# Block order of the last attention's input projection: q0 q1 s0 q2 s1 q3 s2 s3 in place of q0 s0 q1 s1 q2 s2 q3 s3

## What is computed

```
h = rms_norm_2(x, od_norm_w)
proj = h @ od_w_in                                  # 2048 -> 4608
q, k, v, gate = split(proj, [2048, 2304, 2560])     # 32 query heads of 64, 4 key/value heads, 32 heads of gates
q = rope(rms_norm_2(q by heads, q_norm_w), pos)     # k the same
o = windowed_attention_with_sinks(q, k, v, sinks)   # window 128: each block of 128 sees itself and the block before
x = x + (o * silu(gate)) @ od_w_out                 # 2048 -> 2048
```

## Time and profile before

| | |
|---|---|
| median of 3 runs | 1894.64 us (1894.14 to 1895.88) |
| profiled execution | 1893.72 us, its span 1891.9 us |
| TensorE busy | 1879.0 us, 99% of the span, granted clock 1.0 |
| VectorE busy | 1256.7 us, 66% |
| ScalarE busy | 999.7 us, 53% |
| last attention | units 557 to 644, about 1555 to 1846 us of the span |

### The profile page before, as it was taken

How to read it: one execution, slowest core, us unless ns; L and a number is a source line. 1 busy time by engine, 2 the same in 40 slices (tenths; PEclk the granted TensorE clock), 3 DMA queues, 4 the chain that set the end, 5 groups by cost and what they waited for, 6 DMA issues and landing times.

```text
span 1891.9 us, 22459 instructions
## 1 busy us (share of the span) xinstructions
PE 1879.0 (99%) x8563; PEld 1546.8 (82%) x8563; DVE 1256.7 (66%) x1847; ACT 999.7 (53%) x1378; POOL 14.4 (1%) x32
## 2 busy tenths in 40 slices
PE   9999999999999999999999999999999999999999
PEld 7888888888888888888888888888888888877777
DVE  6676567676666566665466776755766677767765
ACT  6777554554444344443444455654555555566663
POOL 0001000000000000000000000000000000000000
PEclk9999999999999999999999999999999999999999
DMA  9667764786666666666666786666676687554565
GB/s 326 201 191 179 206 184 135 225 256 191 197 191 194 196 189 190 198 193 195 191 195 193 219 268 192 193 196 178 189 212 192 195 254 219 175 170 150 167 188 173
DMA packets 212363, 375.85 MB, mean 199 GB/s; under 512 B 14672, under 2 KB 35968, under 8 KB 212256
## 3 DMA queue, kind: packets, MB, share of 16 engines
q1 hardware_dynamic: 211008, 371.65, 64.0%
q0 software_dynamic: 816, 2.11, 0.9%
q10 hardware_dynamic: 432, 0.66, 0.1%
HBM read 361.76 MB, written 12.60 MB: 198 GB/s over the span
## 4 chain that ended last, share of the span: by engine, by line
PE 94%; DVE 3%; ACT 2%; issue 1%; DMA 0%; SPq 0%; DVEq 0%; ACTq 0%
PE g L1185 30%; PE g L1187 30%; PE g L1186 30%; PE m L1119 1%; DVE wl L1652 1%; ACT wh L1375 1%; DVE TW L1652 0%; PE ob L1263 0%; DVE st L1661 0%; PE m L1345 0%; PE m L1245 0%; DVE st L1655 0%; ACT A L1513 0%; DVE A L1655 0%; PE m L1127 0%
## 5 line engine op out<-in xcount | busy, mean ns | idle before, releaser
L1652 DVE TENSOR_TENSOR wl<-raw,wh 128x1024 fp32r<-128x1024 f32 (+1 forms) x660 | 802.5, 1217 | 561.4 <-ACT wh L1375 558.6
L1375 ACT ACTIVATE wh<-raw 128x1024 fp32r<-128x1024 f32 (+1 forms) x661 | 696.3, 1054 | 719.0 <-PE g L1187 713.9
L1185 PE MATMUL g<-wh,xh 128*128 128x512 f32 x1886 | 741.8, 393 | 1.9 <-DVE wl L1652 1.9
L1187 PE MATMUL g<-wh,xl 128*128 128x512 f32 x1886 | 734.6, 390 | 0.0
L1186 PE MATMUL g<-wl,xh 128*128 128x512 f32 x1886 | 734.2, 389 | 0.0
L1185 PEld LDWEIGHTS g<-wh,xh 128*128 128x128 f32 x1886 | 354.1, 188 | 80.0 <-DVE wl L1652 4.3
L1187 PEld LDWEIGHTS g<-wh,xl 128*128 128x128 f32 x1886 | 354.0, 188 | 74.2
L1186 PEld LDWEIGHTS g<-wl,xh 128*128 128x128 f32 x1886 | 354.2, 188 | 71.8
L1185 PE MATMUL g<-wh,mh 128*128 128x512 f32 x732 | 287.4, 393 | 1.8 <-DVE wl L1652 1.8
L1187 PE MATMUL g<-wh,ml 128*128 128x512 f32 x732 | 285.1, 389 | 0.0
L1186 PE MATMUL g<-wl,mh 128*128 128x512 f32 x732 | 284.9, 389 | 0.0
(11 more groups left out here) (174 smaller groups left out, 766.1 us busy)
## 6 DMA issues: line engine op xcount, KB each, us to landing
raw<-in_ev_w_in SPq DMA_DIRECT2D x128, 512.0 KB, 4.1
raw<-in_w_in SPq DMA_DIRECT2D x92, 512.0 KB, 4.3
raw<-in_w_gate SPq DMA_DIRECT2D x88, 512.0 KB, 3.9
raw<-in_w_up SPq DMA_DIRECT2D x88, 512.0 KB, 4.0
raw<-in_w_down SPq DMA_DIRECT2D x88, 512.0 KB, 4.5
raw<-in_od_w_in SPq DMA_DIRECT2D x72, 512.0 KB, 3.7
raw<-in_w_out SPq DMA_DIRECT2D x32, 512.0 KB, 4.8
raw<-in_ev_w_out SPq DMA_DIRECT2D x32, 512.0 KB, 4.7
```

Of the source, the lines that this page charges most:

```text
L1185: e.matmul(o, hi[:, kt, c], h, start=first, stop=False)
L1187: last = e.matmul(o, lo[:, kt, c], h, start=False, stop=end)
L1375: return e.activation(o, i, AF.Copy, scale=scale)
L1652: return e.tensor_tensor(o, a, b, op)
```

## The change

The eight blocks behind okv come in the order q0 q1 s0 q2 s1 q3 s2 s3. Block by block, with the units that each takes:

| units | 557-572 | 573-580 | 581-588 | 589-596 | 597-604 | 605-612 | 613-620 | 621-628 |
|---|---|---|---|---|---|---|---|---|
| before | okv, q0 | s0 | q1 | s1 | q2 | s2 | q3 | s3 |
| after | okv, q0 | q1 | s0 | q2 | s1 | q3 | s2 | s3 |

Nothing else is edited. The planner then lays out the rest anew from that order.

```
     block("od_w_in", 0, 2048, 512, every, "X3", "okv")
-    for j in range(4):
-        block("od_w_in", 0, 512 * j, 512, every, "X3", "oq", j)
-        block("od_w_in", 0, 2560 + 512 * j, 512, every, "X3", "og", j)
+    for kind, j in (("oq", 0), ("oq", 1), ("og", 0), ("oq", 2), ("og", 1), ("oq", 3), ("og", 2), ("og", 3)):
+        block("od_w_in", 0, (2560 if kind == "og" else 0) + 512 * j, 512, every, "X3", kind, j)
     out_blocks("od_w_out", every[:8], every[8:], "M5", 4)
```

## The result

| | before | after |
|---|---|---|
| median of 7 runs each, same chip | 1894.64 us (1893.12 to 1896.03) | 1900.99 us (1899.23 to 1903.27) |
| ratio, 95% interval | | 1.0037 (1.0028 to 1.0046) |
| profiled execution, its span | 1893.72 us, 1891.9 us | 1901.84 us, 1898.9 us |

The forecast was 1895.7, within 1890.8 to 1900.3. The time lies on the slower side, 0.7 us outside the range. The head of the page of the changed kernel answers the earlier trace rows: two more instructions on ScalarE, which are the two table loads, and 7.0 us more span.

What follows compares the result with a forecast made beforehand. TensorE, busy 1879.0 of 1891.9 us, was taken to set the time, with at most 6.3 us of waits to win. Terms -3.1 - 1.0 + 3.2 + 1.5 + 0.3 + 0.2 gave +1.1 us: median 1895.7, range 1890.8 to 1900.3.

Steps and rivals of the forecast that it cites:

- Step 1: Units 605 to 612: q2's chain leaves, so TensorE's 2.03 us wait and two smaller ones go: -3.1 us.
- Step 2: Units 621 to 628: q3's chain leaves, and the one wait there, an `oapt` behind q3's rope, goes: -1.0 us.
- Step 3: Units 597 to 604: q2's chain crowds VectorE's queue, making cuts late by 4.3 us, while 1.1 goes: +3.2 us.
- Step 4: Units 613 to 620: q3's chain enters beside quads 3 and 4; middle of two rows, +1.5 us, from 0 to 4.3.
- Step 5: ScalarE around s0 and s1: two more Exp/Silu table loads, 2.6 us, mostly hidden: +0.3 us, from 0 to 2.6.
- rival (c): ScalarE: both new table loads delay exponentials that transposes wait for, 2.6 in place of 0.3: 1898.0 us; chance 0.10.
- Step 6: q1's chain four steps earlier, +0.2 us (0 to 0.5); quads 6 and 7 four units earlier, 0, at best -0.3.
- (a): VectorE's queue crowded twice, at 597 to 604 and 613 to 620, table loads not hidden: +6.2, 1900.8 us; chance 0.20.
- (b): The planner's spreading hides the chains at 597 to 604 and 613 to 620: about -4.7, 1889.9 us; chance 0.15.
- (d): Last attention: the lanes undo the block reordering, nothing moves, 1894.6 us; chance 0.55 together with the forecast.
- TensorE idle above 10 us from 1600 to 1846: Sign that the forecast is wrong, pointing to VectorE's queue crowded twice or worse.
- the new waits at 600 to 604: Sign that the forecast is right: new TensorE waits for `wl` or exponentials there, 3 to 5 us together.

Runs made afterwards that it cites:

- e2: Against before, only q2 goes ahead of s1 (q0 s0 q1 q2 s1 s2 q3 s3): 1894.84 us, ratio 1.0007 to before.
- e3: Against before, only q3 goes ahead of s2 (q0 s0 q1 s1 q2 q3 s2 s3): 1903.62 us, ratio 1.0054 to before.
- e6: Changed kernel, but a quad's scores are said only once the values of the quad two before it are said: 1895.77 us, ratio 1.0009 to before.
- e1: Against before, only q1 goes ahead of s0 (q0 q1 s0 s1 q2 s2 q3 s3): 1893.07 us, ratio 0.9996 to before.
- e7: Changed kernel with scores behind values, and s2's and s3's Silu evacuations waiting until a begun quad's four exponentials are said: 1892.88 us, ratio 0.9996 to before.
- the same three edits of the planner: Scores behind values, Silu outside quads' exponentials, chain's sum half a unit earlier: before's order 1891.81 us, 0.9988; changed order 1890.94 us, 0.9987, both against before.
- e5: Kernel before with the gates' Silu left out, the four evacuations by Copy: 1891.97 us, ratio 0.9993 to before.
- e4: Changed kernel with the gates' Silu left out, the four evacuations by Copy: 1896.27 us, ratio 1.0013 to before.

## Why the prediction was wrong, step by step

**Step 1, q2's chain leaves 605 to 612 (-3.1): right, and too small.** There is no wait at all from 1703 to 1735. All 3.8 are gone from start to start, the 0.6 too that the prediction kept as quad 2's own; quad 2's exponentials are said three units later now (605.0 to 609.0), so its transposes meet another place. e2 shows the same with q2 alone.

**Step 2, q3's chain leaves 621 to 628 (-1.0): right.** The wait at 627 is gone in after and in e3.

**Step 3, q2's chain enters 597 to 604 (+3.2): right in kind, too large.** Three of the four `wl` waits of after (the fourth is q3's, at 617) and the turn's 0.5 are there, 2.6 from start to start against 4.3, and the 1.1 went: +1.5. The 1.0 at unit 601 measured 0.5, the 1.2 at 602 came as 1.6 in two, the 2.0 at 604 as 0.5. Till the norm the walk was good: sum, root and the product were forecast to end at 1683.4, and the product ends at 1682.9. What was too large is the last part: the cut of 604 was to end at 1700.7 and ends at 1699.7 (1698.47 + 1.22 on VectorE), and TensorE, which has waited for q2's turn before it, wants it half a us later than the walk has it.

**Step 4, q3's chain enters 613 to 620 (+1.5): right, 1.5** at units 616 (0.4) and 617 (1.0). It was the middle between two rows, so the exact hit is luck. The 0.7 behind it, at 618, isn't the chain's but the bank's.

**Step 5, two more table loads (+0.3, at most 2.6): this failed.** The loads themselves cost what the row says, 1.28, and the next activation stands 0.01 us behind the load's end (1792.52 + 1.28 to 1793.81). The Trainium skill, ScalarE: Activation LUTs, What ACT_TABLE_LOAD costs, counts a drain of about 1.38 us beside it, which these rows don't show. The 1900.7 that rival (c) works out with it is near the measured time by luck. What failed is the price: it was taken as two loads times a share that shows, for s0 and s1, as those moved. It did not ask where s2 and s3 would stand, of which s3 hadn't moved at all: quads 4 and 5 had moved under them. s2's swap costs 1.6 and s3's 2.3, both with no load added, and the second 1.5 more by the clock: 5.4 where the term has 0.3. The bound of 2.6 was too low, since it counts two loads and not the evacuation between them, nor that a pair of them can stand between one exponential and its transposes. The removal of Silu takes 4.5 us off the changed kernel and some 1.3 off before, each with about 1.7 to either side.

**Step 6, quads 6 and 7 earlier (0, "an earlier end buys nothing"): this failed most.** It asked what an earlier quad would win, and not what it would meet. They come earlier while quads 2 to 5 come later: in before the values of quads 2 to 5 are said at 608.0, 615.1, 621.1 and 628.0, in after at 611.0, 618.1, 625.0 and 632.0. The scores of quads 6 and 7 went from 628.1 and 634.1 to 625.0 and 632.0 (not to 630.1, as four units would have it). So they stand in the same half unit as the values that had been seven and six and a half units clear of them, right ahead of those and in the same bank. With the scores of quad 5 at 618 this costs 0.7 + 1.5 + 1.5 = 3.7 in the trace. The 1.85 at 636 has the same root but not the bank: quad 6's transposes come earlier, and in ScalarE's queue the copy of the last of them stands behind quad 5's gated product, which comes late and waits for its gates. The prediction puts the gates' way through memory at 0, by how late VectorE is; what the later product would meet it did not ask. e6, which says the scores behind the values, takes 5.3 off, the 636 included. The other half of the step, q1's chain four steps earlier, was right at +0.2: 0.14 us are idle from 1645 to 1675, and e1 shows no difference. The prediction says itself that the scores of quads 0 to 5 stay within a step of their places, and leaves it at that: it walked scores, but not exponentials and values, which the planner's `made` and `room` hold back when a chain crowds ahead of them.

The sum with measured terms: -3.8 - 1.0 + 1.5 + 1.5 + (1.6 + 2.3 + 1.5) + 5.6 = +9.2, less the 0.3 at 634 that went, 8.9; the stage is longer by 8.1. The median moved by 6.35. Before's profiled execution lies 0.92 below its median and after's 0.85 above its own, so of the 8.1 us between the times of the two profiled executions 1.8 belong to which runs were profiled. (That this is the stage's 8.1 again is chance: the spans differ by 7.0.)

**The rivals.** (a) gave 1900.8, and 1900.99 came, but it was the wrong mechanism at the right time: VectorE's queue, crowded twice, costs 1.5 + 1.5 and not 3.2 + 4.3, and e6 and e7 win the whole loss back without touching a chain. (b) and (d) fall. (c), the loads, holds as a kind, with its 2.6 for 5.4. Of the signs named, "TensorE idle above 10 us from 1600 to 1846" came, with 12.0; the new waits at 600 to 604 came with 2.6 and not 3 to 5 us; no wait of TensorE for weight loads came, as expected.

## What to carry over

When a planner moves one piece of work, list every item that lags or leads because of it, and look up which buffers its new neighbours share; an item that comes earlier is not free if the one ahead of it in the same bank, or in the same engine's queue, comes later. Price a table load by what stands behind it in its queue, not by its own length: 1.3 us for six loads in one order, 4.5 for eight in another. And ahead of reordering blocks, fix the order inside the clump: with the same three edits of the planner two block orders that lay 0.37% apart come out at 0.9988 and 0.9987, 0.9 us apart.

## What the runs showed of the hardware

- A wait of about 2 us of TensorE is sometimes followed by some 3.4 us at half clock and sometimes not. In after it was, behind 2.10 shown. In e6 the same transposes waited 1.92 and the clock stayed full: the next matmul is shown 0.48 us long, where it is 0.78 in after. The length alone doesn't decide: the 1.87 ahead of unit 609 was followed by full clock in before (the matmul shown 0.50 long) and by half clock in e5 (0.70, and a granted clock of 0.51 from 1717.6 to 1721.0), and behind the 2.8 of e2 the clock stayed full. A wait of 1.77 to 1.78 near 328.5 us, far ahead of the change, is in every profiled execution; the half clock follows it in those of e1, e4, e6 and e7 and in no other. TensorE's timeline in e5, then in e6:

```profile
1717.54 0.70 PE L1185 MATMUL g<-wh,xh 128*128 128x512 f32 x1 [1.87 <-DVE wl L1652]
...
1798.19 0.66 PE L1118 MATMUL m<-small,A 128*128 128x128 f32 x4 [1.92 <-ACT st L1371]
1798.60 0.48 PE L1184 MATMUL g<-wh,mh 128*128 128x512 f32 x1
```

- Such dips go with part of the scatter between runs of one kernel. Of the eleven runs of e7 the six with a mean granted clock of 1.000 have a mean span of 1890.1 us, the five with 0.999 one of 1891.9. For after it is 1898.0 (two runs), 1899.2 (four) and, at 0.998, 1900.6 (one). They don't make the gain of e6: at 0.999 its spans have a mean of 1894.1 (eight runs), 5.1 below after's, though on another chip. What decides whether a wait is followed by a dip stays open.
